# Even mixer: value projections and turns of band values between and behind the scores of the first two attention items, band values in other memory

## What is computed

```python
# A: latent attention, keys and values made from a 128-wide latent
kv = einsum('btr,rc->btc', ckv, w_ukv).reshape(b, t, 8, 64 + 64)
s = einsum('bqhd,bkhd->bhqk', qn, k_nope) + einsum('bqhd,bkd->bhqk', qp, kpe)
out_a = einsum('bhqk,bkhd->bqhd', softmax(s * scale, mask), v)      # chunk-causal, chunks of 64
# B: band attention, q, k, v straight from the input projection, learned bias by distance
s = einsum('bqhd,bkhd->bhqk', q, k) * scale + rel_table[:, rel]
out_b = einsum('bhqk,bkhd->bqhd', softmax(s), v)
out = concatenate([out_a, out_b], -1) @ even_w_out
```

## Time and profile before

| | us |
|---|---|
| median of three runs | 1897.51 |
| lowest and highest run | 1895.84, 1903.65 |
| the profiled execution: its own time, its span | 1903.65, 1903.7 |
| matmul engine (PE) busy in it | 1884.4 (99%) |
| VectorE, ScalarE, GpSimd busy | 1522.1, 1157.6, 303.8 |

### The profile page before, as it was taken

How to read it: one execution, slowest core, us unless ns; L and a number is a source line. 1 busy time by engine, 2 the same in 40 slices (tenths; PEclk the granted TensorE clock), 3 DMA queues, 4 the chain that set the end, 5 groups by cost and what they waited for, 6 DMA issues and landing times.

```text
span 1903.7 us, 38798 instructions
## 1 busy us (share of the span) xinstructions
PE 1884.4 (99%) x15600; PEld 1830.8 (96%) x15600; DVE 1522.1 (80%) x2005; ACT 1157.6 (61%) x2229; POOL 303.8 (16%) x317
## 2 busy tenths in 40 slices
PE   9999999999999999999999999999999999999997
PEld 9999999999668999999999999999997999999997
DVE  7899997774573888999868889997767488999975
ACT  7566666741585566666666666666638565656564
POOL 0002020300353200111111002020336210020202
PEclk9999999999899999999999999999999999999999
DMA  4232322322311122232341322222331222232322
GB/s 162 89 106 95 106 95 101 123 84 79 125 45 45 52 83 95 90 111 90 111 139 34 97 98 96 104 97 99 121 101 57 67 74 103 85 109 91 110 94 72
DMA packets 59043, 177.95 MB, mean 93 GB/s; under 512 B 7073, under 2 KB 11505, under 8 KB 58737
## 3 DMA queue, kind: packets, MB, share of 16 engines
q1 hardware_dynamic: 55504, 166.50, 26.0%
q0 software_dynamic: 2128, 7.80, 1.3%
q10 hardware_dynamic: 1232, 1.16, 0.2%
HBM read 168.26 MB, written 5.36 MB: 91 GB/s over the span
## 4 chain that ended last, share of the span: by engine, by line
PE 94%; DVE 2%; ACT 2%; issue 1%; POOL 1%; DMA 0%; ACTq 0%; POOLq 0%; DVEq 0%
PE psum L847 29%; PE psum L845 29%; PE psum L846 29%; PE psum L1180 1%; PE psum L1166 1%; PE psum L1299 1%; PE psum L1088 1%; PE psum L1143 1%; PE psum L1282 1%; PE psum L1254 1%; DVE xlo L2121 0%; PE psum L1132 0%; DMA x<-in_x 0%; ACT w_hi L698 0%; DVE y L2032 0%
## 5 line engine op out<-in xcount | busy, mean ns | idle before, releaser
L845 PE MATMUL psum<-xhi,w_hi 128*128 128x272 f32 x1632 | 474.3, 291 | 2.1 <-DVE xlo L2121 2.0
L847 PE MATMUL psum<-xhi,w_lo 128*128 128x272 f32 x1632 | 470.9, 289 | 0.0
L846 PE MATMUL psum<-xlo,w_hi 128*128 128x272 f32 x1632 | 469.4, 288 | 0.0
L845 PEld LDWEIGHTS psum<-xhi,w_hi 128*128 128x128 f32 x1632 | 307.3, 188 | 5.5 <-issue 3.0
L846 PEld LDWEIGHTS psum<-xlo,w_hi 128*128 128x128 f32 x1632 | 307.3, 188 | 0.5
L847 PEld LDWEIGHTS psum<-xhi,w_lo 128*128 128x128 f32 x1632 | 306.7, 188 | 0.0
L748 DVE TENSOR_TENSOR w_lo<-w_raw,w_hi 128x1024 fp32r<-128x1024 f32 (+1 forms) x208 | 236.7, 1138 | 64.3 <-ACT w_hi L745 61.7
L846 PE MATMUL psum<-corner,w_hi 128*128 128x272 f32 x864 | 249.9, 289 | 0.0
L847 PE MATMUL psum<-corner,w_lo 128*128 128x272 f32 x864 | 249.8, 289 | 0.0
L845 PE MATMUL psum<-corner,w_hi 128*128 128x272 f32 x864 | 248.7, 288 | 0.0
L745 ACT ACTIVATE w_hi<-w_raw 128x1024 fp32r<-128x1024 f32 (+1 forms) x208 | 206.2, 991 | 39.9 <-PE psum L847 38.4
(11 more groups left out here) (336 smaller groups left out, 4803.7 us busy)
## 6 DMA issues: line engine op xcount, KB each, us to landing
w_raw<-in_w_gate_up SPq DMA_DIRECT2D x172, 512.0 KB, 4.2
w_raw<-in_w_down SPq DMA_DIRECT2D x96, 384.0 KB, 3.4
w_raw<-in_w_down SPq DMA_DIRECT2D x32, 256.0 KB, 2.7
w_raw<-in_even_in SPq DMA_DIRECT2D x16, 512.0 KB, 3.9
w_raw<-in_odd_in SPq DMA_DIRECT2D x10, 512.0 KB, 4.1
w_raw<-in_even_out SPq DMA_DIRECT2D x8, 512.0 KB, 3.5
w_raw<-in_odd_out SPq DMA_DIRECT2D x8, 512.0 KB, 4.5
out_band_kv<-qkvb POOLq DMA_DIRECT2D x1, 2176.0 KB, 10.0
```

What stands on the lines that cost most here:

```text
L845: nc.tensor.matmul(out, s_hi, m_hi, start=first, stop=False, skip_group_check=skip)
L846: nc.tensor.matmul(out, s_hi, m_lo, start=False, stop=False, skip_group_check=skip)
L847: return nc.tensor.matmul(out, s_lo, m_hi, start=False, stop=last, skip_group_check=skip)
```

## The change

Items 0 and 1 of the attention get their scores inside `even_middle`. The new order there is: values 0, 1, 2; scores of item 0; value 3; band turn 0; scores of item 1; value 4, band turn 1; value 5, band turn 2; value 6, band turn 3; band turn 4 (the sample). All five band turns go to bank 7, since banks 0 to 3 belong to the scores now. Each but the first waits until ScalarE has copied the one before it. On ScalarE and VectorE the first two items go in between in the same way; the band copies, `identE` and the split of g+10 stand before the loop, which starts at item 2.

`vB` moves from the rows of `qkvb` to the memory of `w_sum` and `rstd`, which is idle in the mixer. `probsE` and `probsTE` change places, so that nothing that the first two items write lies on `ckv_hi` or `ckv_lo`, which the value projections still read. The waits of ScalarE for the stored band keys and values move behind the attention.

```diff
         probsE = [place("probsE%d" % i, [P, 2, w], F32, at=pr_at + o) for i, (w, o) in
-                  enumerate(((384, 0), (512, 3072), (384, 7168)))]
-        probsTE = [place("probsTE%d" % i, [P, 2, 512], F32, at=pr_at + 10240 + 4096 * i) for i in range(2)]
-        vB = place("vB", [P, 4, NH * HD], F32, at=arena + 17408)
+                  enumerate(((384, 7168), (512, 10240), (384, 0)))]
+        probsTE = [place("probsTE%d" % i, [P, 2, 512], F32, at=pr_at + o) for i, o in enumerate((3072, 14336))]
+        vB = place("vB", [P, 4, NH * HD], F32, at=w_sum_at)
...
-                    if n < 2:
-                        pe.wait_ge(vb_copied, 2 * n + 2)
-                    else:
-                        pe.wait_ge(exp_done, n - 1)
+                if n == 0:
+                    pe.wait_ge(k_copied, 8)
+                    pe.wait_ge(roped, 6)
+                elif n >= 2:
+                    pe.wait_ge(exp_done, n - 1)
...
-                for n in range(N_EVEN + 4):
+                for n in range(2, N_EVEN + 4):
                     if n < N_EVEN:
-                        scores(n)
+                        even_scores(n)
...
-                pe.wait_ge(roped, 6)
-                for v in range(7):
+                def value(v):
                     cols = slice(v * P, (v + 1) * P)
                     if v >= 3:
                         pe.wait_ge(v_copied, v - 2)
                     mm3(psum[:, 4 + v % 3, :], ckv_hi[:, cols], ckv_lo[:, cols],
                         w_hi[:, slot(g + 1, 1), 0:512], w_lo[:, slot(g + 1, 1), 0:512], True, True).then_inc(v_ready, 1)
-                    if v == 3:
-
-                        pe.wait_ge(k_copied, 8)
-                        for j in range(5):
-                            n = P if j < 4 else DEC
-                            for f in range(4):
-                                mm = nc.tensor.transpose(psum[0:n, j if j < 4 else 7, f * P:(f + 1) * P],
-                                                         qkvb[:, 8 + f, j * P:j * P + n], ident[:])
-                        mm.then_inc(vb_turned, 1)
-                pe.wait_ge(k_copied, 8)
+
+                def band_turn(j):
+
+                    n = P if j < 4 else DEC
+                    if j > 0:
+                        pe.wait_ge(vb_copied, j)
+                    for f in range(4):
+                        mm = nc.tensor.transpose(psum[0:n, 7, f * P:(f + 1) * P], qkvb[:, 8 + f, j * P:j * P + n], ident[:])
+                    mm.then_inc(vb_turned, 1)
+
+                pe.wait_ge(w_lo_done, splits_at(g + 1) + 2)
+                for v in range(3):
+                    value(v)
+                even_scores(0)
+                value(3)
+                band_turn(0)
+                even_scores(1)
+                for j in range(1, 4):
+                    value(3 + j)
+                    band_turn(j)
+                band_turn(4)
                 pe.wait_ge(mask_ready, 1)
...
+            def band_values(j):
+
+                act.wait_ge(vb_turned, j + 1)
+                if j < 4:
+                    nc.scalar.activation(vB[:, j, :], psum[:, 7, :], ACT.Copy).then_inc(vb_copied, 1)
+                    return
+                act.wait_ge(latents_stored, 16)
+                nc.scalar.activation(vB_new[0:DEC, :], psum[0:DEC, 7, :], ACT.Copy).then_inc(vb_copied, 1)
+
+            exponentials(0)
+            band_values(0)
+            exponentials(1)
+            for j in range(1, 5):
+                band_values(j)
+            nc.scalar.activation(identE[:], ident[:], ACT.Copy).then_inc(mask_ready, 1)
+            split_group(act, "act", g + 10)
+            for n in range(2, N_EVEN + 4):
...
+                for v in range(3):
+                    value(v)
+                maxima(0)
+                value(3)
+                invert(0)
+                maxima(1)
+                for v in range(4, 7):
+                    value(v)
+                split_group(dve, "dve", g + 10)
+                for n in range(2, N_EVEN + 5):
```

More of the change, by code:

```diff
@@ new lines, in add, with sample_scores @@
+            def add(rows, b, cols, q, k):
+                return nc.tensor.matmul(psum[rows, b, cols], q, k, start=False, stop=True, skip_group_check=True)
+            def sample_scores(stage, bank, i):
+                new, old, both = slice(0, DEC), slice(DEC, SK), slice(0, SK)
+                if stage == "band":
+                    pe.wait_ge(rel_low, 1 + i)
+                    pe.wait_ge(band_in, 16 * 2)
+                    nc.tensor.matmul(psum[:, bank, both], identE[:], relS_hi[:, i, :], start=True, stop=True)
+                    add(slice(0, P), bank, both, identE[:], relS_lo[:, i, :])
+                for part in range(2):
+                    for d in range(4):
+                        e, p = d % 2, 2 * i + d // 2
+                        rows, r = slice(32 * d, 32 * d + 32), slice(64 * e, 64 * e + 64)
+                        if stage == "band" and part == 0:
+                            add(rows, bank, new, qkvb[r, p, SEQ:T], qkvb[r, 4 + p, SEQ:T])
+                        elif stage == "band":
+                            mm = add(rows, bank, old, qkvb[r, p, SEQ:T], kB_cache[r, p, :])
+                        elif part == 0:
+                            nc.tensor.matmul(psum[rows, bank, both], qN[r, p, SEQ:T], kN[r, p, SEQ:KEYS_A],
+                                             start=True, stop=True)
+                        else:
+                            mm = add(rows, bank, both, qR[rows, i, SEQ:T], kpe_all[rows, SEQ:KEYS_A])
+                return mm
@@ new lines, in even_scores @@
+            def even_scores(n):
+                k, i = EVEN_ITEMS[n]
+                stage, sample, p, _, _ = EVEN[k]
+                bank = 2 * (n % 2)
+                if n == 0:
[3 more added lines that the diff above has]
+                    pe.wait_ge(exp_done, n - 1)
+                if sample:
+                    for half in range(2):
+                        mm = sample_scores(stage, bank + half, half)
+                    mm.then_inc(s_ready, 1)
+                    return
+                at = even_place(n)
+                if stage == "band":
+                    first = True
+                    for b, c, w in even_parts(n):
@@ L1141, in scores @@
                         for e in range(2):
                             r = slice(64 * e, 64 * e + 64)
[L1143 to L1149, removed]
@@ L1150, in scores @@
-                    mm.then_inc(s_ready, 1)
+                            mm = nc.tensor.matmul(psum[:, bank + e, at + c:at + c + w], qkvb[r, p, P * b:P * (b + 1)],
+                                                  qkvb[r, 4 + p, 0:w], start=first, stop=True, skip_group_check=True)
+                        first = False
+                    mm.then_inc(s_ready, 1)
+                    return
+                halves = [(b, half, at + c, w - 64 + 64 * half) for b, c, w in even_parts(n) for half in range(2)]
@@ new lines, in even_scores @@
+                for i, (b, half, c, w) in enumerate(halves):
+                    q, rows = P * b + 64 * half, slice(64 * half, 64 * half + 64)
+                    for e in range(2):
+                        r = slice(64 * e, 64 * e + 64)
+                        nc.tensor.matmul(psum[rows, bank + e, c:c + w], qN[r, p, q:q + 64], kN[r, p, 0:w],
+                                         start=i < 2, stop=True, skip_group_check=True)
+                for b, half, c, w in halves:
+                    q, rows = P * b + 64 * half, slice(64 * half, 64 * half + 64)
+                    for e in range(2):
+                        r = slice(64 * (p % 2) + 32 * e, 64 * (p % 2) + 32 * e + 32)
+                        mm = add(rows, bank + e, slice(c, c + w), qR[r, p // 2, q:q + 64], kpe_all[r, 0:w])
@@ L2459, in rel_part, with value @@
                                                 ALU.subtract).then_inc(rel_low, 1)
-                for n in range(N_EVEN + 5):
+                def value(v):
+                    dve.wait_ge(v_ready, v + 1)
+                    nc.vector.tensor_copy(vA[:, v, :], psum[:, 4 + v % 3, :]).then_inc(v_copied, 1)
+                for v in range(3):
[8 more added lines that the diff above has]
+                for n in range(2, N_EVEN + 5):
                     if n < N_EVEN:
@@ L2563, in _ @@
                         rotate(j, raw, kpe_all[:, HALF[H]] if j < 2 else raw)
[L2564 to L2569 removed]
+                    even_dve(g)
                 else:
```

28 lines of the change are left out of this document (8 added, 20 removed).

## The result

| | before | after |
|---|---|---|
| median, 16 runs each | 1895.79 us | 1902.96 us |
| lowest, highest | 1895.03, 1903.65 | 1899.67, 1908.79 |
| busy PE in the profiled execution | 1884.4 | 1875.8 |

The ratio is 1.0033, with a 95% interval of 1.0022 to 1.0044: slower by 4 to 8 us, small but clear. PE is busy for less time in the profile after only because the same work ran at full clock there; the kernel does the same matmuls. Two things moved. The lowest runs differ by 4.6 us. And the runs spread more: of the 16 of before, nine lie within 0.9 us of 1895.03 and one is above 1900; of the changed kernel six lie within 1.0 us of 1899.67, three at 1901.76 to 1903.20, and seven at 1906.05 and above. The profiled execution of the change is one of the lowest, 1899.67 us (span 1897.9).

The account below looks back on a forecast made before the run. The matmul engine, busy 99% of the span, was taken as the bound, so only idle and low clock mattered. +3.3 - 1.4 + 1.5 = +3.4 us on the median 1,897.51 gave 1,900.9 us, range 1,895.0 to 1,908.0.

Parts of the forecast that it names:

- Items 0 and 1 early, without a stall: Scores among the value tiles: item 0 starts at 491.29 us, item 1 ends at 496.95, matmuls 4.0 us earlier, no wait.
- rival 4: Scores of item 0 wait for keys or rotation and everything slides together: 1,897.5 us as before; chance 0.03.
- Band turns through one bank, +3.3: Bank 7: idle of 1.8 us before turn 2, 0.65 before turn 4, 0.95 for `identE`; item 2 starts 3.3 us later.
- The hole that was aimed at, -1.4 and +1.5: Item 3's wait for item 1's exponentials goes (-1.4 us); item 4 waits for item 2's, behind the split (+1.5).
- The sum, +3.4: Whole edited stretch at equal clock: +3.3 - 1.4 + 1.5 = +3.4 us, 3.0 to 3.9 with hand-overs.
- The base: Profiled execution taken as 1,903.65 us, near 1,894.2 without its 9.5 us low-clock loss; differences carried to median 1,897.51.
- rival 2: The clock holds and the holes stay: 1,903.65 - 9.5 + 3.4 = 1,897.6 us; chance 0.24.
- The clock, "as much low clock as before": Matmul engine's clock in the attention: the middle between falling by 504.25 us and never falling, with 9.5 us staying away.
- Rival 1: Holes in front of item 2 bring the clock down and it stays down, +3.8 us: 1,907.4; chance 0.24.
- The rule that spoke against the change: Skill rule: short matmul-engine idles between groups cycling through PSUM make the clock swing; turn, copy, turn in one bank match.
- Rival 3: Bank 7 doesn't hold the engine up, item 2 starts before 502.3 us, the clock holds: 1,892.8 us; chance 0.07.

Follow-up runs that it names:

- experiment 4: Changed kernel with band turns in banks 7, 0, 1, 7, 5, split of g+10 before item 0's exponentials, `identE` before the exp table; median 1895.01 us, ratio to before 0.9975.
- Experiment 3: Changed kernel with the band turns in banks 7, 0, 1, 7, 5 instead of 7 alone; median 1898.07 us, ratio to before 1.0007.
- Experiment 2: Changed kernel with the split of g+10 back beside the value tiles, ahead of item 0's exponentials; median 1899.21 us, ratio to before 1.0003.
- experiment 7: Kernel before with 12 unused transposes filling the hole ahead of item 3's scores; median 1895.99 us, ratio to before 0.9995.
- experiment 6: Changed kernel with the copy of band turn 1 ahead of item 1's exponentials on ScalarE; median 1902.43 us, ratio to before 1.0031.
- experiment 5: Changed kernel with only `identE` moved, ahead of the exp table again; median 1907.19 us, ratio to before 1.0052.
- experiment 8: Changed kernel with 14 unused transposes filling the idle ahead of item 4's scores; median 1900.66 us, ratio to before 1.0020.
- 9: Changed kernel with unused transposes ahead of band turns 2, 3, 4 (13, 1, 5) and the `identE` wait (7); median 1905.86 us, ratio to before 1.0037.
- experiment 1: Kernel before with the four changed buffer addresses alone; median 1896.80 us against 1897.57, ratio 0.9997.

## Why the prediction was right, and where it was off

**The forecast** was 1,900.9 and no difference that counts; measured 1902.96, inside the range, with a ratio of 1.0033. The mechanism of the waits was the right one, at the places named. But the number is closer than the working deserves. The forecast difference was +3.4 us and the medians differ by 7.2; the forecast missed by only 2.1 us because I added 3.4 to a median of three runs (1897.51), where that of 16 runs is 1895.79. That part is luck.

- *Items 0 and 1 early, without a stall*: right. Item 0 starts 2.18 us after the first value tile (predicted 2.09), and the exponentials of item 1 end 3.0 us after its scores. That settles rival 4 too.
- *Band turns through one bank, +3.3*: mis-sized, **+4.1** measured (15.81 against 11.70). The waits are near the predicted ones: 1.53 for 1.8, 0.69 for 0.65, 0.88 for 0.95. Of the 0.8 us that were missing, 0.24 is there before turn 2 (11.64 us after the first value tile, 11.40 by my sum). I had put the new order itself at nothing ("the moved tiles change no instruction"); experiment 4 shows it at 0.5 us without any listed wait. Another 0.43 comes between turns 2 and 4, since I left out the drain of a turn. I charged 0.44 for the transposes and 0.60 for the copy, 1.1 with hand-overs; but turn 2 starts at 499.89, copy 2 at 500.58, turn 3 at 501.23, turn 4 at 502.57. A turn and its copy in one bank take 1.34 us, because the copy waits 0.69 from the turn's start. So turn 3 waited too, for a copy that I had at just in time. Experiment 3 shows it from the other side: other banks win 2.6 us.
- *The hole that was aimed at, -1.4 and +1.5*: right in kind; 1.44 went and 1.68 came. Experiment 2 removes it by moving the split alone.
- *The sum, +3.4*: **+4.35** at equal clock, by experiment 7.
- *The base*: I took the profiled execution for the run of 1,903.65, as the table ahead of the prediction does. In the runs of the change the time is 1.8 us over the span (1899.67, 1897.9), and it is 1.8 to 1.9 in those of every experiment, so by this estimate a span of 1903.7 belongs to about 1905.5. The cost of the low stretch was nearly right: I had 9.5, and the span without it, in experiment 7, is 9.3 shorter. But rival 2's 1,897.6 was then 2 too low from this, and 1 more from the sum: the lowest runs are at 1,899.7 to 1,900.6.
- *The clock, "as much low clock as before"*: this step failed. The change brought it down more often: seven long runs of 16 against one of 16. Its median is 3.3 over its lowest run, that of before 0.8 over its own, so some 2.5 of the 7.2 us are clock. I had the nearest row, the hole among score matmuls, in both kernels, and one more group of holes in the new one, and still took them for equal.
- *Rival 1 (1,907.4)*: seven of 16 runs are in its place by their time, but its mechanism, a fall ahead of item 2, fits only one of them. Where the clock fell ahead of item 2 (experiment 6) the mean clock of the run is 0.992; where it fell behind the hole ahead of item 4 (experiment 5), 0.995. Of the seven runs one has 0.992 (1908.79) and six have 0.994 or 0.995. So the hole ahead of item 4, which rival 1 took for closed, fits most of them; that is read from the mean clock and not from a trace of these runs.
- *Rival 2 (1,897.6)*: six runs kept the clock up (mean clock 0.998), but lie 2 us and more above its figure, for the two reasons above, and so near the forecast's own number by accident. The outcome is two or three heaps, and the median of 1902.96 stands between them.
- *The rule that spoke against the change*: the rule of the Trainium skill, "TensorE: Matmul & The Clock Gate", section "A second HAM failure mode: psum-queue depth-cycling", pointed the right way. In the trace of experiment 6 only the idle at the turns and the wait for `identE` lie ahead of the fall, and the same holds for the runs of 1902.90 to 1904.30 in experiment 8, by their time. No run separates the idle in the one bank from the wait for `identE`.
- *Rival 3* failed at the condition that it names. Experiment 4 meets it, with the split moved as well, and stands at 1,895.0; rival 3's 1,892.8 would be 1,894.6 with the base put right.

What stays open: what decides in a single execution whether the clock falls. The same hole of 1.67 or 1.68 us left it at 1.00 in the profiled executions of the change and of experiments 3 and 9. Only the profiled executions show when the clock fell, and no long run of the changed kernel was profiled. That the runs of 1,902.9 to 1,904.3 in experiment 8 are a shorter low stretch is read from their time and mean clock (0.996 to 0.997, against 0.998 in the others), not from a trace.

## What to carry to other kernels

Work that is moved to fill a wait brings its own waits: look at the bank it needs, at what stands ahead of its copy on an engine that works in order, and at what it pushes back there. Turn, copy and turn in one bank cost the drain as well; use the banks that are free at that moment. Mixing kinds of work has a price of its own, here 0.5 us. Where matmuls are small and the engine must idle for a microsecond or two, judge by many runs, and try dummy full-array work in the hole: here that alone narrowed the spread from 3.7 to 1.0 us (experiment 7).

## What the runs showed of the hardware

- In four profiled executions the clock fell, 0.2 to 1.2 us after the end of an idle piece: at about 504.7 behind 1.44 us among scores (before), at 504.6 behind 1.44 (experiment 1), at 511.3 behind 2.42 (5), and at 503.6 behind 0.88 at `identE` (6). It did not fall behind 1.68, 1.67 and 1.68 us in three others (the change, 3, 9).
- Long runs in one set: none of 24 with 0.16 us ahead of item 4 (experiments 2 and 4), 11 of 47 with 1.44 ahead of item 3 (before and 1), five of 12 with 1.67 ahead of item 4 (3). In the other sets before had 1 of 16, 0 of 19 and 2 of 20. With 2.42 all five lie 6 us above the lowest of the change (5). Experiments 2, 3 and 5 had idle at the turns or `identE` as well.
- Once down it stayed for 14 to 24 us with the engine busy all the time: from 504.7 to 525.2 before, from 504.6 to 521.7 in experiment 1, from about 511.3 to 524.9 in experiment 5 (0.91 and 0.89 in the outer stretches), from 503.6 to 527.5 in experiment 6 (0.95 and 0.56). In all four, scores, turns and values ran without a gap at 1.2 GHz.
- From the start of four 128x128 float32 transposes to the start of the copy that waits for them: 0.69 us. A value tile on another bank followed the transposes of turn 2 after 0.41 us.
- The first matmul of a value tile behind scores or turns took 0.31 to 0.34 us until the next one started, behind another value tile 0.23 to 0.24 (the change and experiment 4).
